# Expert weights as two 512 KB transfers per tile, each half waited for, released and replaced alone

## The reference

```python
aff = jax.nn.sigmoid(jnp.matmul(xt, w_router).astype(jnp.float32))
...
_, e_idx = lax.top_k(jnp.where(e_keep, sel, -jnp.inf), TOP_K)      # 2 of 16 experts per token
...
def expert_block(args):
    xb, e = args
    gate, up = jnp.split(jnp.matmul(xb, w_up[e]), 2, axis=-1)      # 1024 -> 2 x 512
    return jnp.matmul(jax.nn.silu(gate) * up, w_down[e])           # 512 -> 1024
...
e = jnp.matmul(p[i], ple_proj[i]) * jax.nn.sigmoid(jnp.matmul(h, ple_gate[i]))
m = moe_ffn(h, w_router, router_bias, exp_w_up[i], exp_w_down[i])
h = layer_norm_2(DEEPNORM_ALPHA_2 * h + m + e, ln2_g[i], ln2_b[i])
```

## Time and profile before

| what | value |
|---|---|
| median of 3 runs | 1462.78 us (1461.36 to 1464.81) |
| profiled execution, its own time | 1461.82 us |
| its span | 1460.1 us |
| granted TensorE clock, mean | 0.993 |
| TensorE busy | 98% of the span |
| VectorE, ScalarE busy | 63%, 48% |
| moved by DMA | 333.78 MB, mean 229 GB/s |
| expert loads of 1 MB | 96, and 4 in pieces |

### The profile page before, as it was taken

The page is one execution under the profiler, slowest core; times in us unless marked ns, Lnnn a source line. Parts: engine busy times, 40 slices in busy tenths (PEclk is TensorE's granted clock), DMA queues, the critical chain, the costliest instruction groups (busy, mean ns, idle before and its releaser), DMA issues.

```text
span 1460.1 us, 20759 instructions
## 1 busy us (share of the span) xinstructions
PE 1426.5 (98%) x8400; PEld 1162.2 (80%) x8400; DVE 915.8 (63%) x1505; ACT 704.7 (48%) x1169; POOL 51.7 (4%) x116
## 2 busy tenths in 40 slices
PE   8999999999999999999999999998999999999995
PEld 7888888888888988889898988888899997445441
DVE  7666578766676765567668666668989685121123
ACT  7455456454554644545755545445546553112211
POOL 0000000000000000000022000001000030000000
PEclk9999999999999999999999999999999999999998
DMA  8754554565555555444345755543554379999997
GB/s 345 283 197 173 200 204 145 202 231 177 198 182 193 202 195 205 177 155 177 131 150 211 252 177 198 191 173 137 174 184 143 137 305 405 376 409 421 419 421 288
DMA packets 50198, 333.78 MB, mean 229 GB/s; under 512 B 5808, under 2 KB 6064, under 8 KB 12208
## 3 DMA queue, kind: packets, MB, share of 16 engines
q1 hardware_dynamic: 48512, 322.55, 58.8%
q10 hardware_dynamic: 1584, 9.83, 1.8%
HBM read 331.31 MB, written 1.05 MB: 228 GB/s over the span
## 4 chain that ended last, share of the span: by engine, by line
PE 89%; DVE 4%; ACT 2%; POOL 2%; DMA 1%; SPq 1%; issue 1%; DVEq 0%; POOLq 0%; ACTq 0%
PE psw L603 55%; PE psy L603 31%; PE psw L606 2%; DVE wlo L1927 1%; SPq L2871 1%; DMA hold<-in_we 1%; ACT whi L1360 1%; POOL r L2790 0%; DVE x L2019 0%; DMA ar<-in_xT 0%; DVE xs L1936 0%; DVE x L2032 0%; ACT gb L1482 0%; DVE r L2001 0%; POOL rstd L2748 0%
## 5 line engine op out<-in xcount | busy, mean ns | idle before, releaser
L603 PE MATMUL psw<-xs,whi 128*128 128x512 f32 (+2 forms) x2160 | 648.1, 365 | 6.4 <-DVE wlo L1927 6.4
L1927 DVE TENSOR_TENSOR wlo<-raw,whi 128x1024 fp32r<-128x1024 f32 (+4 forms) x415 | 477.3, 1194 | 75.0 <-ACT whi L1360 69.9
L603 PE MATMUL psw<-xs,wlo 128*128 128x256 f32 x1848 | 483.4, 280 | 0.1
L603 PEld LDWEIGHTS psw<-xs,whi 128*128 128x128 f32 (+1 forms) x2160 | 374.2, 188 | 61.4 <-DVE wlo L1927 6.4
L1360 ACT ACTIVATE whi<-raw 128x1024 fp32r<-128x1024 f32 (+4 forms) x415 | 402.3, 1024 | 7.6 <-PE psy L603 5.2
L603 PEld LDWEIGHTS psw<-xs,wlo 128*128 128x128 f32 x1848 | 348.9, 189 | 17.6 <-DVE wlo L1927 0.6
L1360 ACT ACTIVATE hf<-psw 128x256 f32<-128x256 f32 x90 | 33.9, 383 | 211.7 <-PE psw L603 211.7
L1972 DVE TENSOR_TENSOR hf<-hf,psw 128x256 f32<-128x256 f32 x82 | 34.0, 420 | 146.0 <-ACT hf L1360 146.0
L1360 ACT ACTIVATE ar<-psw 128x256 f32<-128x256 f32 (+2 forms) x141 | 60.1, 430 | 125.9 <-PE psw L603 121.9
L603 PE MATMUL psy<-whi,hhi 128*128 128x512 f32 x352 | 111.2, 390 | 0.0
L603 PE MATMUL psy<-whi,hlo 128*128 128x512 f32 x352 | 111.0, 389 | 0.0
(11 more groups left out here) (347 smaller groups left out, 1790.7 us busy)
## 6 DMA issues: line engine op xcount, KB each, us to landing
raw<-in_ws SPq DMA_DIRECT2D x189, 1024.0 KB, 4.8
hold<-in_we SPq DMA_DIRECT2D x47, 1024.0 KB, 11.0
raw<-in_we SPq DMA_DIRECT2D x22, 1024.0 KB, 10.4
ar<-in_we SPq DMA_DIRECT2D x20, 1024.0 KB, 12.2
gb<-in_ln ACTq DMA_DIRECT2D x7, 1024.0 KB, 5.2
raw<-in_ws SPq DMA_DIRECT2D x9, 768.0 KB, 4.2
raw<-in_ws SPq DMA_DIRECT2D x4, 672.0 KB, 3.9
raw<-in_ws SPq DMA_DIRECT2D x8, 256.0 KB, 6.8
```

Of the source, the lines that this page charges most:

```text
L603: return e.matmul(o, l, rr, start=start, stop=stop)
L1927: e.tensor_tensor(wlo[i % NS][:, c0:c1], raw_t[slot[i]][:, c0:c1], whi[i % NS][:, c0:c1].bitcast(f32), ALU.subtract).then_inc(*made.up((i, ...
```

## The change

Each 1 MB tile is loaded by two transfers of 512 KB (columns 0 to 1023, then 1024 to 2047), each with a semaphore of its own. A step of TensorE waits for the first halves of its tiles, works on them, signals `("used", ..., 0)`, waits for the second halves, works on them and signals `("used", ..., 1)`. SP issues the first half of a tile when the first half of the slot's former tile has been used, then waits for the second. The gate tiles wait for both halves ahead of their first matmul and give both back together. The four `halved` tiles keep their transfers of 512, 256 and 256 KB.

```diff
-        slot_in = [Signal(sem(f"s_slot{i}"), 16) for i in range(WSLOTS + len(ONCE))]
+        slot_in = [Signal(sem(f"s_slot{i}"), 16) for i in range(2 * (WSLOTS + len(ONCE)))]
...
+                def landed(n, j, h):
+                    for q in job_columns(n):
+                        i = enumber[v][n, q, j]
+                        need.wait_ge(*slot_in[2 * i_slot(v, i) + h].at("we", v, i, h))
...
                     for k in (2 * j, 2 * j + 1):
+                        landed(n, j, k % 2)
                         for z in range(2):
                             for p0, p1, w in ws:
                                 ins = mm(...)
-                    ins.then_inc(*s.pe.up(("used", v, n, j), *([("up", v, n)] if j == 3 else [])))
+                        ins.then_inc(*s.pe.up(("used", v, n, j, k % 2), *([("up", v, n)] if j == 3 and k % 2 else [])))
...
                     for k in range(4):
+                        if k % 2 == 0 and not (halved(v, n, j) and k):
+                            landed(n, j, k // 2)
...
+                        if k == 1:
+                            ins.then_inc(*s.pe.up(("used", v, n, j, 0)))
-                    ins.then_inc(*s.pe.up(("bank", ("ey", v, n, i)), ("used", v, n, j)))
+                    ins.then_inc(*s.pe.up(("bank", ("ey", v, n, i)), ("used", v, n, j, 1)))
...
+                def given_back(h):
+                    if turn_of.get(g, 0) >= WSLOTS:
+                        v_, i_ = esequence[ring[turn_of[g] - WSLOTS]]
+                        need.wait_ge(*(over if v_ else main).pe.at("used", v_, *[etiles[v_][i_][m] for m in (0, 2)], h))
...
-                if halved(v, n, j):
-                    e.dma_start(wslots[at][:, 0:LATE[0]], src[:, 0:LATE[0]]).then_inc(*slot_in[at].up(("we", v, i)))
-                else:
-                    e.dma_start(wslots[at], src).then_inc(*slot_in[at].up(("we", v, i)))
+                for h in range(1 if halved(v, n, j) else 2):
+                    if h:
+                        given_back(1)
+                    e.dma_start(wslots[at][:, D * h:D * h + D], src[:, D * h:D * h + D]).then_inc(*slot_in[2 * at + h].up(("we", v, i, h)))
```

More of the change, by code:

```diff
@@ L1147, in gate_part @@
                 i = enumber[0]["gate", 0, c]
-                need.wait_ge(*slot_in[i_slot(0, i)].at("we", 0, i))
+                for h in range(2):
+                    need.wait_ge(*slot_in[2 * i_slot(0, i) + h].at("we", 0, i, h))
                 w = blocks(wslots[i_slot(0, i)], T)
@@ L1154, in gate_part @@
                 if t:
-                    ins.then_inc(*pe.up(("bank", ("pleg", c)), ("used", 0, "gate", c)))
+                    ins.then_inc(*pe.up(("bank", ("pleg", c)), ("used", 0, "gate", c, 0), ("used", 0, "gate", c, 1)))
             turned(7, 0)
@@ L1196, in job @@
                     return JOBS * v + n
+                def landed(n, j, h):
+                    for q in job_columns(n):
+                        i = enumber[v][n, q, j]
+                        need.wait_ge(*slot_in[2 * i_slot(v, i) + h].at("we", v, i, h))
                 def weights_in(n, q, j, width=D):
-                    i = enumber[v][n, q, j]
-                    need.wait_ge(*slot_in[i_slot(v, i)].at("we", v, i))
-                    return blocks(wslots[i_slot(v, i)], width)
+                    return blocks(wslots[i_slot(v, enumber[v][n, q, j])], width)
                 def gather(G):
@@ L1855, in take @@
                     if (v, n, i) == (0, 0, 0):
-                        need.wait_ge(*pe.at("used", 0, 0, 5))
+                        need.wait_ge(*pe.at("used", 0, 0, 5, 1))
                     copy(y_hi[:, 512 * i:512 * i + 512], place["ey", v, n, i][:, :]).then_inc(*s.act.up(("yhi", v, n, i)))
@@ L2884, in load_expert @@
                 elif turn_of[g] >= WSLOTS:
-                    v_, i_ = esequence[ring[turn_of[g] - WSLOTS]]
-                    need.wait_ge(*(over if v_ else main).pe.at("used", v_, *[etiles[v_][i_][m] for m in (0, 2)]))
+                    given_back(0)
                 elif wslot_after[turn_of[g]] is None:
@@ L2944, in sync @@
             n, _, j = etiles[0][ONCE[3]]
-            need.wait_ge(*pe.at("used", 0, n, j))
+            need.wait_ge(*pe.at("used", 0, n, j, 1))
             e.dma_start(gbv, A["ln"][8:9, :].broadcast_to((128, 2 * D))).then_inc(*last_in.up(("gb", 8)))
```

## The result

The changed kernel takes 1466.88 us in the median (12 runs, 1465.12 to 1469.78), the kernel before on the same chips 1462.64 us (12 runs, 1460.81 to 1464.81). The ratio is 1.0031, its 95% interval 1.0023 to 1.0038: slower by 4.2 us, where +3.7 us (1466.5) was forecast. The profiled execution has a span of 1464.4 us, against 1460.1.

What follows compares the result with a forecast made beforehand. The DMA engines were taken to bound the stage from 1254.70 us on. Packets +4.9 and restart -1.2 sum to +3.7 us, a predicted 1466.5 us; the 8-in-10 range is 1462.3 to 1470.0.

Steps and rivals of the forecast that it cites:

- What sets the end: TensorE paces the loads up to 1254.70 us; from there to 1446.9 the DMA engines set the end.
- The transfers, +4.9: From 1254.70 us on, 70 tiles in 4096-byte runs cost 0.07 us more each: +4.9 us (3.5 to 8.4).
- Rival 1: The packets cost only 0.05 us per tile at full queue: +2.3 us in all, 1465.1; chance 0.22.
- The restart, -1.2: At 1254.70 us, where loading resumes after the hole, the early first half gains 1.2 us; bounds 0 to 1.25.
- Earlier releases of half slots at all later places bring nothing, since the queue never runs empty again.: Behind the restart, giving half slots back earlier gains 0 us, because loads are always queued.
- Rival 2: Halves released earlier fill slow stretches after the restart, such as 1275 to 1280, saving 3.0 us: +0.7, 1463.5; chance 0.17.
- Extra packets ahead of the hole cost nothing.: Tiles ahead of 1254.70 us pay for packets too, but the extra ends in the hole (2.5 us at share 0.31).
- Issues hidden.: SP's 70 more issues of 0.33 us make about 1.1 us per tile, hidden under the 2.5 us of its bytes.
- Rival 3: SP's queue blocks at about ten transfers in flight, issues take 2 us, the stage grows by 133 us; chance 0.02.
- rival 4: Each second half pays a lone load's 2.3 us start even in a queue: +161 us; chance 0.01.
- TensorE waits for nothing new.: Added waits and signals in five steps up to 1254.70 us could delay the restart by 0.5 us; taken as nothing.
- The tail, 13 us.: Behind the last landing, some 13 us (1460.1 less 1446.9) stay as they are.

Runs made afterwards that it cites:

- e3: Kernel before with expert weights laid out half by half: one 1 MB transfer per tile in 4096-byte packets, gate tiles unchanged, slots given back whole; 1467.92 us, ratio 1.0029.
- e4: Four transfers of 256 KB per tile (2048-byte packets), slots given back whole, against the kernel before; 1481.85 us, ratio 1.0131.
- e9: The kernel before, unedited, profiled a second time; 1463.30 us.
- e10: The kernel before, unedited, profiled a third time; 1464.34 us.
- e6: Changed kernel with halves only for 20 ring tiles (sixteenth to thirty-fifth), all others whole; 1463.28 us, ratio 1.0000 to the kernel before.
- e5: Changed kernel with the tiles that fill empty slots loaded whole, only replacements of used tiles in halves; 1467.34 us, ratio 1.0033 to the kernel before.
- e1: Changed kernel without early release: both halves issued after the whole former tile is used, both awaited before a step's first matmul; 1468.49 us, ratio 1.0036 to the kernel before.
- e7: Changed kernel with two and three unread matmuls added ahead of the last step's waits for late pieces; 1467.69 us, ratio 1.0032 to the kernel before.
- e8: The changed kernel, unedited, profiled a second time; 1466.85 us.
- e11: The changed kernel, unedited, profiled a third time; 1467.41 us.
- e2: Like the split-only kernel, but each tile's two transfers cut by partitions (64 each), keeping 8192-byte packets; 1655.60 us, ratio 1.1314 to the kernel before.

## Why the prediction was right, and where its steps were not

**What sets the end.** Right. Between the last milestones the difference hardly moves (+3.2 at the last 1 MB tile, +3.3 at the last piece), and the end moves with the rate of the bytes in e3 and e4. In e9 TensorE was still at work for 1.5 us behind the last landing, and the end came no later for it (13.4 us).

Two readings ahead of the sum were off, without harm to it. "Stands at 405 to 421" passes over the slice of 376 GB/s, from 1241 to 1278 us, which holds the hole. And "TensorE waits once for 3.3 us on a tile" leaves out two more waits for loads, all three in the last job:

```profile
PE psw L603 <- DMA ar<-in_we: 1.9, 1, 1.9
PE psw L603 <- DMA hold<-in_we: 0.9, 1, 0.9
```

**The transfers, +4.9.** Right. 4.7 by the windows of three profiles each, 2.556 against 2.49 by the landings of one. e3 adds what the trace before couldn't show: it is the packet's price, paid by one transfer of 1 MB as well. Rival 1 (0.05) falls short. The Trainium skill's estimate, 0.03 us a tile by "DMA: Bandwidth & Descriptors", section "Why small descriptors are slow (HBM only)", is less than half of the 0.067 measured.

**The restart, -1.2.** This is the step that failed. The first half was issued when it should be (1253.19, forecast 1252.9). But "the second half, issued at 1254.70, lands at 1254.70 + 2.3 + 1.25 = 1258.25" is wrong: it was issued at 1254.90 and landed at 1261.6. Two things were missed.

First, the hole was spent twice: it was to swallow the extra of the tiles ahead ("the extra ends in that hole") and to take the early half as well. In the changed kernel the tile ahead of the restart is whole at 61.9 to 62.3 us (four profiles) and the first half lands 1.2 us behind it, at 63.2 to 63.5. At 1.28 us for each half the second can't be there before 64.5 to 64.8, and the kernel before has its whole tile at 64.5 to 64.7. There was nothing to gain. In e9 and e10 the tile ahead of the restart is as late as that (61.8 and 62.0) without small packets, and the restart's tile still lands at 64.5 and 64.7, so the wide hole of the first profile was no sign of time that could be won.

Second, the second half comes later than that: 2.9, 3.0 and 3.5 us behind the first in three of the four profiles, 1.25 in the fourth, and 4.1, 4.9 and 5.1 in e6, e5 and e1. The prediction's sum, a lone load's start of 2.3 us and the half's own 1.25, has no term for this. By that landing the changed kernel is 1.1 us behind in the mean of three profiles (1.4 with e7's), not 1.2 ahead.

**"Earlier releases of half slots at all later places bring nothing, since the queue never runs empty again."** The reason given is wrong: "not empty" is not enough. With two to four tiles in flight the kernel before still has landings that come 0.9, 0.8 and 1.3 us late, at 72.9, 83.7 and 87.5 us. The lost time puts numbers to the parts, from runs that have one without the other:

| kernel | transfers for each tile | slot given back | lost time, us |
|---|---|---|---|
| before (three profiles) | 1 | whole | 6.3, 5.3, 6.5 |
| e3_one_transfer_4k | 1, small packets | whole | 5.8 |
| e1_split_only | 2 | whole | 7.6 |
| e4_quarters | 4 | whole | 7.9 |
| changed (three profiles, and e7) | 2 | by halves | 4.5, 4.3, 4.7, 5.8 |
| e5_fill_whole | 2, replacements only | by halves | 4.5 |
| e6_early_ring | 2, for 20 tiles | by halves for these | 5.1 |

Read as it stands, more transfers lose 1.6 to 1.9 us more (7.6 and 7.9 against a mean of 6.0), and giving back by halves is worth 2.8 against that (7.6 to a mean of 4.8). This split is an estimate: 7.6, 7.9, 5.8 for e3, 4.5 and 5.1 each rest on a single profile, and profiles of one kernel differ by up to 1.4 us. The net is -1.5, or -1.2 with e7's profile. The forecast had -1.2 from another place, with a landing that came 3.3 us later than it said. So the packets were right, the second term was right in size by luck, and the total with it.

**Rival 2** (finer releases fill the later gaps) named the place, and its mark, no slow stretch behind 1260, is half there: 394, 405 and 394 GB/s from 1262 to 1300 before, 411, 405 and 406 after. It put the lost time at 4.2 us less; 1.2 to 1.5 were had. e1 has the mark too, without the finer releases, so the mark doesn't show that they are the cause.

**Extra packets ahead of the hole cost nothing.** Right for the end, by e5; that they leave less of the hole to the early half is told above.

**Issues hidden.** Right. In this stretch of SP's timeline in the changed kernel, at full queue,

```profile
1406.81 13.11 SPq L2923 DMA_DIRECT2D hold<-in_we  x11
```

11 issues take 13.11 us, 1.2 each, with some 12 halves in flight (15.8 us to landing at 1.28 each). SP is then paced by the landings and holds nothing up: the share stays at 1.03. Rival 3 is refuted, and rival 4 too at full queue (1.278 us for each half, not 1.28 + 2.3).

**TensorE waits for nothing new.** Right up to the last job: the restart's slot is used up at 59.6 to 59.7 us in all six profiles, so the added waits and signals cost nothing that can be seen. The waits of the changed kernel for tiles, from 1194 us on (total, times, longest), answer to the earlier trace rows:

```profile
PE psy L603 <- DMA hold<-in_we: 4.5, 1, 4.5
...
PE psw L603 <- DMA hold<-in_we: 3.4, 3, 1.6
...
PE psw L603 <- DMA ar<-in_we: 1.2, 1, 1.2
```

All of them lie in the last job.

**The tail, 13 us.** Right in five profiles of six (13.2 to 13.5), 14.5 in one. TensorE's timeline in the changed kernel shows its last two waits for late pieces:

```profile
1447.38 0.59 PE L603 MATMUL psw<-ar,kT 128*32 128x512 f32 x1 [1.27 <-DMA hold<-in_we]
...
1450.00 1.03 PE L603 MATMUL psw<-ar,kT 128*32 128x512 f32 x1 [1.55 <-DMA hold<-in_we]
```

The clock in the window behind was 0.50. The same came in e5:

```profile
1448.61 0.59 PE L610 MATMUL psw<-ar,kT 128*32 128x512 f32 x1 [1.20 <-DMA hold<-in_we]
...
1451.93 1.03 PE L610 MATMUL psw<-ar,kT 128*32 128x512 f32 x1 [2.26 <-DMA hold<-in_we]
```

In these two profiles TensorE waited for over 1 us twice within the last 5 us ahead of the eight matmuls. In the others it waited once (0.6 to 1.3 us) or not at all for these pieces, and the eight ran at 1.00. Whether the change makes the double wait more frequent is open: it was seen in two of eight profiles with smaller packets (the changed kernel's first and e5; not in e1, e3, e4, e6, e8, e11) and in none of the three of the kernel before.

**What stays open.** Why a second half lands late in a shallow queue. It came with two transfers (e1 against e3, one profile each) and also where the first fill came whole (e5); no run shows the mechanism, and it was not measured alone. One more candidate stands in the traces: the DMA view of the changed kernel from 1254 to 1256 us has one packet of the instruction queue (0.02 MB) among the loads,

```profile
q8 instruction: 1, 0.02, 3.2%
```

and the kernel before has one in the same place (58.7 us into the stage), where the tile landed 4.8 us after its issue. No run moves it. How much of the lost time the early release saves, and how much goes once the loads run late, is open too. The 0.5 us between the medians' +4.2 and the spans' +3.7 is inside the interval (3.4 to 5.6 us).

## What to carry to other kernels

Where a stage is set by the DMA engines at full queue, price a split by its packets, from a transfer of that size in the trace: here 8.4 to 8.8 ns for each packet on each engine, the same with one transfer for a tile as with two. Finer releases can bring something only where few loads are queued, so try a split there alone, and count what the extra transfers lose there; here 20 tiles in halves brought about what they cost. A hole in the traffic can be spent only once: look whether the loads ahead of it will grow into it, and whether it is there in a second profile. A stretch where the queue "never runs empty" can still be slow: compare its GB/s with the best window, not its share with 1.

## What the runs showed of the hardware

- Packets of 8192, 4096 and 2048 bytes to 128 partitions move 420, 409 and 387 GB/s at a full queue (e3 and e4 against before). At 4096 bytes the rate is the same with one transfer for a tile (e3) as with two (e1, the changed kernel).
- Transfers to 64 partitions move 229 GB/s even when the queue is full of them (e2).
- When SP's queue holds some 12 transfers of 512 KB, an issue takes 1.2 us instead of 0.33 and follows the landings. It delayed nothing here: the DMA share stayed at 1.03.
- At the restart, with few loads queued, the second of two transfers of 512 KB landed 1.25 to 5.1 us behind the first (1.28 at a full queue), 4.8 to 8.8 us after its issue; one of 1 MB landed 4.8 to 5.2 us after its issue.
